# Three gate/up chunks of each feed-forward stage by seven block products, with two of the weight sums made by accumulating DMAs

## The reference

```python
def swiglu(x, w_gate, w_up, w_down):
    return (jax.nn.silu(x @ w_gate) * (x @ w_up)) @ w_down

for i in range(DEPTH):
    x = x + 0.5 * swiglu(rms_norm(x, norm_g[i, 0]), ffn_gate[i, 0], ffn_up[i, 0], ffn_down[i, 0])
    ...
    x = x + 0.5 * swiglu(rms_norm(x, norm_g[i, 2]), ffn_gate[i, 1], ffn_up[i, 1], ffn_down[i, 1])
```

## Time and profile before

| | us |
|---|---|
| median of 3 runs | 3238.48 (3237.65 to 3241.2) |
| the profiled execution, device time | 3234.98 |
| its span | 3233.2 |
| PE busy | 3160.3 (98% of the span), 15659 matmuls |
| DVE busy | 2356.6 (73%) |
| ACT busy | 1684.8 (52%) |
| POOL busy | 181.4 (6%) |
| mean clock granted to TensorE | 0.995 of full speed |
| moved by DMA | 576.19 MB, 52.3% of what the 16 engines' time holds on the main queue |

### The profile page before, as it was taken

How to read it: one execution, slowest core, us unless ns; L and a number is a source line. 1 busy time by engine, 2 the same in 40 slices (tenths; PEclk the granted TensorE clock), 3 DMA queues, 4 the chain that set the end, 5 groups by cost and what they waited for, 6 DMA issues and landing times.

```text
span 3233.2 us, 38895 instructions
## 1 busy us (share of the span) xinstructions
PE 3160.3 (98%) x15659; PEld 2622.6 (81%) x15659; DVE 2356.6 (73%) x2822; ACT 1684.8 (52%) x2033; POOL 181.4 (6%) x297
## 2 busy tenths in 40 slices
PE   7999999979999999999999999999999999999998
PEld 6888888867888887888888888887788788977887
DVE  6877878776778775468778778655687787655786
ACT  5544555555555545345545555465555555565554
POOL 0000000022000003000000000012100000122000
PEclk9999999989999999999999999999999999999999
DMA  6555645533646556555455555654465654744553
GB/s 228 182 183 195 222 132 207 182 101 123 221 140 218 187 181 202 184 207 195 153 183 208 186 196 182 190 158 131 143 215 181 206 195 144 197 131 137 195 182 127
DMA packets 315855, 576.19 MB, mean 178 GB/s; under 512 B 45401, under 2 KB 114092, under 8 KB 315548
## 3 DMA queue, kind: packets, MB, share of 16 engines
q1 hardware_dynamic: 313148, 566.71, 52.3%
q0 software_dynamic: 2384, 6.64, 0.8%
q10 hardware_dynamic: 144, 0.35, 0.0%
HBM read 571.53 MB, written 1.09 MB: 177 GB/s over the span
## 4 chain that ended last, share of the span: by engine, by line
PE 87%; DVE 7%; ACT 4%; issue 1%; DMA 1%; POOL 0%; SPq 0%; DVEq 0%; ACTq 0%
PE up L2160 15%; PE up L2162 14%; PE up L2161 14%; PE acc L2160 8%; PE acc L2162 8%; PE acc L2161 8%; PE up L2618 4%; PE up L2619 4%; PE up L2620 4%; DVE w_lo L1227 3%; ACT w_hi L657 2%; PE up L2596 1%; DVE xT_lo L1344 1%; ACT xT_hi L731 1%; DVE x L1294 0%
## 5 line engine op out<-in xcount | busy, mean ns | idle before, releaser
L1227 DVE TENSOR_TENSOR w_lo<-raw,w_hi 128x2048 fp32r<-128x2048 f32 (+1 forms) x455 | 1031.3, 2270 | 577.2 <-ACT w_hi L657 574.7
L657 ACT ACTIVATE w_hi<-raw 128x2048 fp32r<-128x2048 f32 (+1 forms) x455 | 864.8, 1902 | 755.5 <-PE up L2162 411.1
L2160 PE MATMUL up<-w_hi,xT_hi 128*128 128x512 f32 (+2 forms) x1916 | 756.6, 395 | 16.0 <-DVE xT_lo L1344 5.0
L2162 PE MATMUL up<-w_hi,xT_lo 128*128 128x512 f32 (+2 forms) x1916 | 745.6, 389 | 0.0
L2161 PE MATMUL up<-w_lo,xT_hi 128*128 128x512 f32 (+2 forms) x1916 | 744.9, 389 | 0.0
L2160 PE MATMUL acc<-w_hi,ff_hi 128*128 128x512 f32 x1232 | 486.5, 395 | 1.2 <-DVE ff_lo L1812 1.2
L2162 PE MATMUL acc<-w_hi,ff_lo 128*128 128x512 f32 x1232 | 480.2, 390 | 0.0
L2161 PE MATMUL acc<-w_lo,ff_hi 128*128 128x512 f32 x1232 | 479.6, 389 | 0.0
L657 ACT ACTIVATE w_hi<-arena 128x2048 fp32r<-128x2048 f32 x154 | 295.0, 1916 | 283.2 <-PE up L2162 153.1
L2160 PEld LDWEIGHTS up<-w_hi,xT_hi 128*128 128x128 f32 x1916 | 360.5, 188 | 96.5 <-DVE w_lo L1227 13.1
L2162 PEld LDWEIGHTS up<-w_hi,xT_lo 128*128 128x128 f32 x1916 | 360.4, 188 | 74.1
(11 more groups left out here) (367 smaller groups left out, 3766.7 us busy)
## 6 DMA issues: line engine op xcount, KB each, us to landing
raw<-in_ffn_down SPq DMA_DIRECT2D x88, 1024.0 KB, 5.2
raw<-in_ffn_gate SPq DMA_DIRECT2D x52, 1024.0 KB, 5.1
raw<-in_ffn_up SPq DMA_DIRECT2D x52, 1024.0 KB, 5.2
raw<-in_ffn_wi SPq DMA_DIRECT2D x48, 1024.0 KB, 5.2
raw<-in_ffn_wo SPq DMA_DIRECT2D x44, 1024.0 KB, 7.5
raw<-in_w_in SPq DMA_DIRECT2D x38, 1024.0 KB, 5.1
arena<-in_ffn_wi SPq DMA_DIRECT2D x32, 1024.0 KB, 7.9
arena<-in_ffn_gate SPq DMA_DIRECT2D x28, 1024.0 KB, 7.8
```

What stands on the lines that cost most here:

```text
L657: nc.scalar.activation(w_hi[n % RING][:, 0:c], source(n)[:, 0:c], ACT.Copy).then_inc(hi_ready, 1)
L1227: nc.vector.tensor_tensor(w_lo[n % RING][:, 0:c], source(n)[:, 0:c], w_hi[n % RING][:, 0:c].bitcast(F32), ALU.subtract).then_inc(lo_ready, 1)
L2160: pe.matmul(ps, lh, rh, start=start, stop=False)
L2162: return pe.matmul(ps, ll, rh, start=False, stop=stop)
```

## The change

Chunks 2, 3 and 4 of each fast stage are now all made by seven block products. In each of them T1 and T3 are no longer DVE instructions. T1: SP loads B12, then GpSimd's queue issues a DMA that reads B11 from HBM and adds it into the same buffer. T3: once tile B11 is split, GpSimd's queue loads B12 again into B11's buffer, waits for it, and issues a second DMA that adds B22 into it. T2 and T4 stay on DVE. The four block buffers change roles from chunk to chunk (`BLOCKS_IN`), so that the blocks of the next chunk can be loaded as buffers come free; SP's queue waits for the tile and the sum that free each. The order of products is B11, T1, B22, T2, B21, T3, T4, with the down and tail tiles put between them as the list in `tiles_of` says. A stage has 42 tiles. At its end the last chunk's transposes come between the two token halves of tile 39, and only tiles 40 and 41 are left for the two passes over the token halves. `PAR` gives the halves of `ff_hi` and `ff_lo` that a chunk uses. ACT's queue is reordered in the same way as DVE's, which is shown; the functions `take_v`, `take_c12`, `take_c22` and `take_c21` hold the same DVE instructions as `fast` did, and `product_1` to `product_7` the same block products with the same waits. `free(n)` is SP's wait until tile n is split, and with a second argument also until so many sums are done.

```diff
@@ -26,7 +26,10 @@
 NFC = FF // FW
 
 
-BLOCK_OF = {"B11": 0, "B21": 2, "T1": 0, "B22": 3, "T2": 0, "T3": 1, "T4": 2}
+ROLE_OF = {"B11": 0, "T1": 1, "B22": 3, "T2": 1, "B21": 2, "T3": 0, "T4": 1}
+BLOCKS_IN = ((0, 1, 2, 3), (2, 3, 0, 1), (0, 1, 2, 3))
+CHUNKS = (2, 3, 4)
+PAR = (0, 1, 0, 0, 1, 1)
 STEPS_OF = {"v": 1, "u": 2, "c12": 3, "c22": 4, "w": 5, "c21": 6}
 
 QUARTERS = 4
...
@@ -416,13 +419,17 @@
                 if s in fast_stages:
                     downs = [down_tile(wd, FW * (j // 2) + CW * (j % 2)) for j in range(2 * NFC + 1)]
 
-                    def chunk(spacers):
-                        b11, b21, t1, b22, t2, t3, t4 = [(4, FW, None, name) for name in BLOCK_OF]
-                        return [b11, spacers[0], b21, t1, spacers[1], b22, t2, spacers[2], t3, spacers[3], t4]
-
-                    t = wide(wg, 0) + wide(wu, 0) + wide(wg, 1) + wide(wu, 1) + chunk(downs[0:4])
-                    t += wide(wg, 3) + wide(wu, 3) + chunk(downs[4:7] + [tail(0)])
-                    return t + [tail(1)] + downs[7:11]
+                    def part(k):
+                        return [(4, FW, None, name, len(CHUNKS) * fast_stages.index(s) + k) for name in ROLE_OF]
+
+                    t = wide(wg, 0) + wide(wu, 0) + wide(wg, 1) + wide(wu, 1)
+                    b11, t1, b22, t2, b21, t3, t4 = part(0)
+                    t += [b11, downs[0], t1, downs[1], b22, t2, b21, t3, t4, tail(0), tail(1), downs[2]]
+                    b11, t1, b22, t2, b21, t3, t4 = part(1)
+                    t += [b11, downs[3], t1, downs[4], b22, t2, b21, t3, downs[5], t4]
+                    b11, t1, b22, t2, b21, t3, t4 = part(2)
+                    t += [b11, t1, downs[10], b22, t2, b21, downs[6], t3, t4]
+                    return t + [downs[j] for j in (7, 8, 9)]
                 t = wide(wg, 0)
                 for c in range(NFC):
                     t += wide(wu, c) + (wide(wg, c + 1) if c + 1 < NFC else [tail(0), tail(1)])
...
             def blocks_before(s, n0, j):
 
+                q = len(CHUNKS) * fast_stages.index(s)
                 if j == 9:
                     sp.wait_ge(scale_ready, seen.next(scale_ready))
+                    load_block(s, 0, 0)
+                    load_block(s, 0, 1)
+                elif j == 11:
+                    sp.wait_ge(S_summed, seen.next(S_summed, 4))
+                    load_block(s, 0, 2)
+                elif j == 17:
+                    sp.wait_ge(S_lo_ready, seen.next(S_lo_ready))
+                    load_block(s, 0, 3)
+                elif j == 21:
+                    free(n0 + 12, 2 * q + 1)
+                    load_block(s, 1, 1)
+                    free(n0 + 14, 2 * q + 2)
+                    load_block(s, 1, 0)
+                    free(n0 + 15)
+                    load_block(s, 1, 2)
+                    free(n0 + 16)
+                    load_block(s, 1, 3)
+                elif j == 39:
+                    free(n0 + 24, 2 * q + 3)
+                    load_block(s, 2, 1)
+                    free(n0 + 26, 2 * q + 4)
                     load_block(s, 2, 0)
-                    load_block(s, 2, 1)
-                elif j == 12:
-                    sp.wait_ge(S_summed, seen.next(S_summed, 4))
+                    free(n0 + 27)
                     load_block(s, 2, 2)
-                elif j == 15:
-                    sp.wait_ge(S_lo_ready, seen.next(S_lo_ready))
+                elif j == 40:
+                    free(n0 + 29)
                     load_block(s, 2, 3)
...
+                def add_block(k, role, tile):
+
+                    i, j = BLOCKS_IN[k][1], BLOCKS_IN[k][role]
+                    dve.wait_ge(block_in[j], 16 * (q0 + k + 1))
                     dve.wait_ge(lo_ready, tile + 1)
                     nc.vector.tensor_tensor(blocks[i], blocks[i], blocks[j], ALU.add).then_inc(sum_ready, 1)
...
@@ -1531,28 +1568,83 @@
                 dve.wait_ge(S_hi_ready, seen.next(S_hi_ready))
                 nc.vector.tensor_tensor(S_lo[:], S_raw, S_hi[:].bitcast(F32), ALU.subtract).then_inc(S_lo_ready, 1)
                 consumed(n0 + 6)
-                add_block(0, 1, 1, n0 + 8)
                 used()
                 product(1)
                 split_lo(n0 + 7 + RING)
-                fast(n0 + 8, 2)
+
+                consumed(n0 + 8)
+                hidden_lo(1, 2)
+                add_block(0, 3, n0 + 10)
+                consumed(n0 + 9)
+                used()
+                take_v()
+                split_lo(n0 + 10 + RING)
+                consumed(n0 + 11)
+                add_block(0, 2, n0 + 13)
+                consumed(n0 + 12)
+                used()
+                take_c12(0)
+                split_lo(n0 + 13 + RING)
+                consumed(n0 + 14)
+                used()
+                take_c22(0)
+                split_lo(n0 + 15 + RING)
+                used()
+                take_c21(0)
+                split_lo(n0 + 16 + RING)
+                consumed(n0 + 17)
+                hidden_lo(2, 2)
+                used()
+                product(NFC)
+                split_lo(n0 + 18 + RING)
                 consumed(n0 + 19)
-                hidden_lo(2, 2)
-                for j in (20, 21):
-                    consumed(n0 + j)
-                add_block(0, 1, 1, n0 + 23)
+
+                consumed(n0 + 20)
+                hidden_lo(NFC, 1)
+                add_block(1, 3, n0 + 22)
+                consumed(n0 + 21)
                 used()
-                product(3)
+                take_v()
                 split_lo(n0 + 22 + RING)
-                fast(n0 + 23, 4)
+                consumed(n0 + 23)
+                add_block(1, 2, n0 + 25)
+                consumed(n0 + 24)
                 used()
-                hidden_lo(4, 2)
-                product(NFC)
+                take_c12(1)
+                split_lo(n0 + 25 + RING)
+                consumed(n0 + 26)
+                used()
+                take_c22(1)
+                split_lo(n0 + 27 + RING)
+                consumed(n0 + 28)
+                used()
+                take_c21(1)
+                split_lo(n0 + 29 + RING)
+
+                add_block(2, 3, n0 + 31)
+                consumed(n0 + 30)
+                hidden_lo(3, 2)
+                used()
+                take_v()
+                split_lo(n0 + 31 + RING)
+                consumed(n0 + 32)
+                add_block(2, 2, n0 + 34)
+                consumed(n0 + 33)
+                used()
+                take_c12(2)
                 split_lo(n0 + 34 + RING)
                 consumed(n0 + 35)
-                hidden_lo(NFC, 1)
-                late.extend([n0 + 36, n0 + 37])
...
-                fast(n0 + 8, 2, lambda n: down(n, 1, 1))
+
+                product_1(n0 + 8)
+                prodded()
+                turn_hidden(1, 4)
+                hidden_done(2)
+                down(n0 + 9, 0, 0)
+                pe.wait_ge(S_lo_ready, seen.next(S_lo_ready))
+                product_5(n0 + 10)
+                down(n0 + 11, 0, 1)
+                product_3(n0 + 12, 0)
+                hidden_done(2)
+                product_6(n0 + 13)
+                product_2(n0 + 14)
+                product_7(n0 + 15, 0)
+                product_4(n0 + 16)
                 pe.wait_ge(c11_gated, seen.next(c11_gated))
-                half_pair(n0 + 19, 0, gates)
+                half_pair(n0 + 17, 0, gates)
+                prodded()
                 turn_hidden(2, 4)
-                half_pair(n0 + 20, 1, gates)
-                pe.wait_ge(ff_lo_ready, seen.next(ff_lo_ready, 2))
-                pair(n0 + 21, ups_)
-                pe.wait_ge(ff_gated, seen.next(ff_gated, 2))
-
-                def tail_first(n):
-                    pe.wait_ge(c11_gated, seen.next(c11_gated))
-                    half_pair(n, 0, gates)
-
-                fast(n0 + 23, 4, tail_first)
-                half_pair(n0 + 34, 1, gates)
+                half_pair(n0 + 18, 1, gates)
+                down(n0 + 19, 1, 0)
+
+                prodded()
+                product_1(n0 + 20)
+                hidden_done(2)
+                turn_hidden(NFC, 2)
+                down(n0 + 21, 1, 1)
+                product_5(n0 + 22)
+                down(n0 + 23, 2, 0)
+                product_3(n0 + 24, 1)
+                hidden_done(1)
+                product_6(n0 + 25)
+                product_2(n0 + 26)
+                product_7(n0 + 27, 1)
+                down(n0 + 28, 2, 1)
+                product_4(n0 + 29)
+
+                pe.wait_ge(c11_gated, seen.next(c11_gated))
+                product_1(n0 + 30)
+                prodded()
+                turn_hidden(3, 4)
+                product_5(n0 + 31)
+                down(n0 + 32, NFC, 0)
+                product_3(n0 + 33, 2)
+                hidden_done(2)
+                product_6(n0 + 34)
+                product_2(n0 + 35)
+                down(n0 + 36, 3, 0)
+                product_7(n0 + 37, 2)
+                product_4(n0 + 38)
+
```

(111 more changed lines are left out.)

175 lines of the change are left out of this document (69 added, 106 removed).

## The result

The changed kernel takes 3331.73 us (median; 3325.39 to 3333.77), the kernel before beside it 3238.85 (3237.65 to 3241.2): a ratio of 1.028, 95% interval 1.0265 to 1.030. The forecast was 3315 us, range 3258 to 3384, slower: size and sign held. The profiled execution took 3325.39 us; its span, 3323.6 us, is 90.4 us longer than before's 3233.2.

What follows compares the result with a forecast made beforehand. PE's own work was taken as the bound. Per stage 9.6 us of waits less 2.7 of work, 7.0 when carried on, times 11 gave +77: 3312 for the profiled execution, 3315 us for the median, range 3258 to 3384.

Steps and rivals of the forecast that it cites:

- The removed product: Chunk 3 of each fast stage: 84 matmuls instead of 96, 2.72 us less PE work a stage, 29.9 us over 11 stages.
- The `c12` wait: Chunks 2 and 3: DVE's queue delivers `c12` at 10.3 us, PE needs it at 8.2; PE waits 2.1 us in each.
- The later waits: PE waits of 1.2 (tile 30), 0.6 (`v`), 0.6 (split of 36), 1.9 (tile 39) and 1.1 us (`ff_lo`) a stage.
- the layout: DVE, ACT and PE queues laid side by side, instructions starting when engine and waits allow; error under 0.5 us a stage.
- The moved transfers: T1 and T3 sums by GpSimd's DMA: hidden, costing nothing; chunk 4 tightest, 12 us of room for a 10 us transfer.
- the upper bound of 18.8: Accumulating DMA's longest assumed time, twice a slower plain block; at it, 6 us more a stage, +66 in all.
- The clock: PE's granted clock read as full speed, 2.4 GHz, in nearly every slice of the earlier profile; no term for it.
- 1 (late transfers): Rival: accumulating transfers for T1 and T3 arrive late, adding 66 us, 3381 us; chance 0.20.
- 2 (faster): Rival: DVE's queue isn't late, `c12` falls inside 8.2 us, so the kernel takes 3209 us; chance 0.06.
- 3: Rival: only the two `c12` waits are real, the later ones not; 3255 us; chance 0.11.
- 4: Rival: chunk 3 keeps its length, its products fed no faster, and the waits stay; 106 us more, 3344; chance 0.05.

Runs made afterwards that it cites:

- the run with four orders: Changed kernel with the sum earlier, transposes moved, stage end reordered, and chunk 4's sum T4 behind tile 36's split: 3226.91 us, 0.9971 of before.
- the swap of the sum: Changed kernel with DVE making sum T4 of chunks 2 and 3 ahead of the split of tile 14 (26): 3276.07 us, 1.0121 of before.
- The run with the end alone: Changed kernel with DVE's `c21` step ahead of tile 40's split and the hidden block's low part ahead of tile 41's split: 3298.86 us.
- the run with the transposes alone: Changed kernel with PE's transposes behind tile 30 moved after tile 31's product, and ACT's copy of tile 32 ahead of the SiLU: 3323.53 us.
- the run without them: Changed kernel with GpSimd's DMAs for T1 and T3 left out, only signals kept, plain blocks used instead: 3333.39 us.
- the run with filled waits: Changed kernel with eight unread matmuls ahead of the product that waits for `c12` at tiles 13 and 25: 3313.12 us.

## Why the prediction was right, step by step

From start to start, in one stage of after (378.65 to 568.38), less the pitch of 0.227:

| place | forecast | measured |
|---|---|---|
| `c12`, chunks 2 and 3 | 2.1, 2.1 | 2.02, 2.02 |
| tile 30, before the transposes | 1.2 | 1.24 |
| `v`, tile 33 | 0.6 | 0.44 |
| split of tile 36 | 0.6 | 0.43 |
| tile 39, before the transposes | 1.9 | 2.22 |
| `ff_lo`, end | 1.1 | 0.85 |
| slower first matmul behind five waits | not counted | 0.5 |
| sum | 9.6 | 9.7 |

Less 2.7 us of block products that is +7.0; the stage grew by 189.7 - 182.5 = 7.2.

- **The removed product**: right. 132 matmuls fewer. The 2.7 us could be had only where PE doesn't wait, and the run with four orders got 0.8 of them. DVE's work in a stage grew by 151.8 - 148.1 = 3.7 us, not by the 6 of the forecast, which entered no term of the sum.
- **The `c12` wait**: right, in place, count and size, and the swap of the sum shows the cause: the sum T4 and its place in the queue.
- **The later waits**: right in place; the single sizes are off by up to 0.3 us and cancel in the sum. The run with the end alone and the run with the transposes alone took two groups of them away. Without the low clock they are worth 3.0 and 1.3 us a stage, where the layout had 3.1 and 1.2. The waits for `v` and for the split of tile 36 had no run of their own. The forecast of some 100 us more idle time of PE came out as 87 by the page, whose idle column is 0.16 us too small for each wait.
- **The moved transfers**: at nothing, right, shown by leaving them out. ACT's copies of T1 and T3 waited for no DMA; twice in the run a copy of chunk 4's tile B11 did (2.8 and 4.1 us), with PE's waits there as elsewhere. The step's inner size was wrong: in chunk 4, the tightest, the room from T1's issue to its copy was 18.7 us in the first stage and not 12. Block B12 was loaded at 130.65 and GpSimd's command followed at 136.05, 5.4 us later, where the forecast took 9.4 and 1 for that, and the copy came 1.7 us later than laid out, as much as the low clock behind this stage's `c12` wait costs. In the second stage, where the clock stayed up, the room is 437.18 - 420.21 = 17.0 us. T1 took 8.5 us there where I took 10, but up to 16.0 in chunk 2, under the upper bound of 18.8 (the longest of all 66). The Trainium skill (Collectives: The Full Stack, The bandwidth ceiling) says of the reduce step of a collective that the engines' add needs two source reads, which halves the rate. These traces have the direction right and leave the factor open: against the plain reload of the same chunk the accumulating block took 2.0 and 1.9 times as long in chunk 2, 1.6 and 2.0 in chunk 3, 1.3 and 1.5 in chunk 4, each beside other transfers. The 18.8 that the forecast made of the rule, twice a block of 9.4, was not reached.
- **The clock**: not foreseen. I had read the earlier trace rows as a clock at full speed and carried it over. It adds 18.5 us to the profiled execution, and 5 us less of it elsewhere bring that to 13.4: 77.0 + 13.4 is the 90.4 measured. It is most of the 17 us between the forecast's 3315 and the median; that the time still fell well inside the range owes nothing to this step. The median lies 6 us above that execution, with a mean clock of 0.988 and 0.989 in the other runs against 0.991. So it is probably also why the runs lie 8 us apart; the other executions have no trace to show it.
- **Rivals**: 1 (late transfers) is out by the run without them. 2 (faster) asked for DVE's queue to be in time; it wasn't, but 2.2 us in the right place make it so, and then the kernel is faster by 10 us, not by 30. 3 and 4 are out: every wait was there, and no product took longer than before.

What stays open: why 11 of 22 equal waits were followed by the lower clock and 11 weren't. Of the eleven waits of 1.8 to 2.1 us at tile 39 none has it in the changed kernel, one in the run with the sum earlier, and none in the run with filled waits. I ran nothing that varies this.

## What to carry to other kernels

When a change removes matmuls from a kernel bound by PE, lay the in-order queues side by side before trusting any share of busy time: DVE was 80% busy and still late in four places, since each of its steps is bound to the tile used three before. Then ask of each wait which instruction ahead of it in the queue nobody needs yet; here four moves of one or two lines were worth 105 us. A wait of 2 us can cost nearly twice its length when the clock falls behind it, so on a kernel bound by PE a wait that can't be removed is worth filling; here that gave back 18.6 us.

## What the runs showed of the hardware

- After an idle stretch of PE of 1.86 us the granted clock went to the lower level for about 3.4 us, in 11 of 22 cases; filled with matmuls, in none. Each cost 1.7 us: eleven of them 18.5 by the slices, and the filled run was 18.6 us faster.
- Differences between executions of this size go with that clock. The changed kernel and the one without transfers differ by 8.3 us in the span of their profiled executions (3323.6 and 3331.9) and by 8.3 us in the slices of low clock (27.1 and 35.4). The three executions of the changed kernel with a mean clock of 0.988 and 0.989 took 6 to 8 us more than the one with 0.991.
- An accumulating DMA of 1 MiB from HBM into SBUF took 9.5 and 11.5 us (medians of 33), a plain one from the same queue between them 6.7. What else was under way mattered as much: the same command took 8.5 us in chunk 4 and 14.5 in chunk 2 (medians of 11), and in chunk 4, issued again while other loads ran, 15.5.
